# Key/value projection in quarters between the modulation blocks of a two-layer diffusion backbone, with weights stored as tiles

## The reference

```python
sh1, sc1, g1, sh2, sc2, g2 = adaln(c[:, None, :], mod_w[l], mod_b[l])        # silu(c) @ mod_w + mod_b
csh1, csc1, cg1, csh2, csc2, cg2 = adaln(c_ctx, mod_w[l], mod_b[l])
pl = modulate(x, norm_mix_g[l], sh1, sc1) @ w_in                              # latent: q, k, v, conv
hc = modulate(xc, norm_mix_g[l], csh1, csc1)
pc = hc @ (w_in if ctx_full else w_in[:, KV_LO:KV_HI])                        # context: k and v only
...
h = jnp.sin(f_freq * (h @ f_w2 + f_b2)); h = h @ f_w3                         # filters of layer 1
window = jnp.exp(-t_norm[:, None] * jnp.abs(f_decay)[None, :]) + FILTER_MOD_SHIFT
kf = jnp.fft.rfft(k2, n=2 * n, axis=0)                                        # their spectrum
```

## Time and profile before

| | us |
|---|---|
| median of 3 runs | 2467.48 (2467.28 to 2470.25) |
| the profiled execution: its own time | 2467.65 |
| its span, first to last instruction | 2465.9 |
| PE busy | 2372.1 (96% of the span) |
| DVE busy | 1823.9 (74%) |
| ACT busy | 1015.1 (41%) |
| start, up to the first product of `U_KV` | 151.24 |
| end of `U_KV` and first product of the next unit | 198.91 |

### The profile page before, as it was taken

One profiled execution on the slowest core, in us unless ns is written; L12 is line 12 of the kernel. 1 busy time (PEld: TensorE's weight loads), 2 busy tenths in 40 slices (PEclk: granted clock), 3 DMA queues, 4 the chain that ended last, 5 costly groups with the idle time before them and its releaser, 6 DMA issues.

```text
span 2465.9 us, 37957 instructions
## 1 busy us (share of the span) xinstructions
PE 2372.1 (96%) x14656; PEld 2073.9 (84%) x14656; DVE 1823.9 (74%) x2439; ACT 1015.1 (41%) x963; POOL 0.2 (0%) x4
## 2 busy tenths in 40 slices
PE   6899799998999999999989999999899999999997
PEld 2369478997888888888889989999788888888887
DVE  3557769988888888888888777875878655665565
ACT  4432334434444444444443223233444444444444
POOL 0000000000000000000000000000000000000000
PEclk7789899998999999999999999999999999999999
DMA  9897178996888888888875566556677555555552
GB/s 355 279 327 284 51 267 326 344 339 242 303 292 312 321 299 302 298 320 316 294 260 183 208 225 220 197 196 211 216 283 267 185 190 203 187 178 194 193 189 102
DMA packets 266042, 613.82 MB, mean 249 GB/s; under 512 B 12208, under 2 KB 12336, under 8 KB 265456
## 3 DMA queue, kind: packets, MB, share of 16 engines
q1 hardware_dynamic: 260992, 602.08, 68.6%
q10 hardware_dynamic: 4912, 9.77, 1.1%
HBM read 605.51 MB, written 6.29 MB: 248 GB/s over the span
## 4 chain that ended last, share of the span: by engine, by line
PE 86%; DVE 6%; DMA 3%; ACT 2%; issue 1%; SPq 0%; DVEq 0%; ACTq 0%
PE acc L578 20%; PE aux L578 20%; PE acc L521 17%; PE acc L604 11%; PE aux L604 10%; PE aux L521 2%; PE aux L656 1%; DMA w_raw<-mod_first 1%; ACT w_hi L1401 1%; PE aux L829 1%; PE aux L850 1%; DMA w_raw<-od_w_in 1%; DMA scr<-k_freq 1%; PE aux L518 1%; DVE w_lo L884 1%
## 5 line engine op out<-in xcount | busy, mean ns | idle before, releaser
L884 DVE TENSOR_TENSOR w_lo<-w_raw,w_hi 128x2048 fp32r<-128x2048 f32 x372 | 849.6, 2290 | 260.1 <-ACT w_hi L1401 244.8
L1401 ACT ACTIVATE w_hi<-w_raw 128x2048 fp32r<-128x2048 f32 x372 | 710.1, 1912 | 625.1 <-PE acc L521 278.1
L578 PE MATMUL acc<-act_a,w_hi 128*128 128x512 f32 x1216 | 295.4, 396 | 6.7 <-issue 4.5
L578 PE MATMUL aux<-act_a,w_hi 128*128 128x512 f32 x1216 | 290.1, 391 | 0.0
L578 PEld LDWEIGHTS acc<-act_a,w_hi 128*128 128x128 f32 x1216 | 226.9, 191 | 53.5 <-issue 5.8
L521 PE MATMUL acc<-act_a,w_hi 128*128 128x256 f32 x1920 | 261.7, 287 | 6.1 <-DVE summed L924 3.6
L578 PEld LDWEIGHTS aux<-act_a,w_hi 128*128 128x128 f32 x1216 | 223.4, 188 | 43.3
L521 PEld LDWEIGHTS acc<-act_a,w_hi 128*128 128x128 f32 x1920 | 247.6, 194 | 9.4 <-issue 4.5
L578 PE MATMUL acc<-act_b,w_hi 128*128 128x512 f32 x1024 | 244.3, 391 | 0.0
L892 DVE SCALAR_TENSOR_TENSOR m_raw<-m_raw,wide 128x1024 f32<-128x1024 f32 x180 | 217.7, 1218 | 5.0 <-DMA m_raw<-mod_rest 4.7
L578 PEld LDWEIGHTS acc<-act_b,w_hi 128*128 128x128 f32 x1024 | 188.2, 188 | 36.4
(11 more groups left out here) (169 smaller groups left out, 2189.2 us busy)
## 6 DMA issues: line engine op xcount, KB each, us to landing
w_raw<-ffn_w SPq DMA_DIRECT2D x256, 1024.0 KB, 7.0
m_raw<-mod_rest SPq DMA_DIRECT2D x180, 512.0 KB, 6.4
scr<-mod_rest SPq DMA_DIRECT2D x140, 512.0 KB, 6.7
w_raw<-od_w_in SPq DMA_DIRECT2D x48, 1024.0 KB, 8.1
w_raw<-ev_w_in SPq DMA_DIRECT2D x36, 1024.0 KB, 9.2
w_raw<-mod_first SPq DMA_DIRECT2D x32, 1024.0 KB, 9.6
w_raw<-ev_w_out SPq DMA_DIRECT2D x16, 1024.0 KB, 10.0
w_raw<-od_w_out SPq DMA_DIRECT2D x16, 1024.0 KB, 5.1
```

The lines of the kernel that those rows point to most:

```text
L578: return pe.matmul(banks[:, ft, :], w_hi[:, kg % 2, kc * 512 + ft * P:kc * 512 + ft * P + P], rhs[:, k, :], start=(k == 0), stop=False)
L884: TT(w_lo[:, kg % 2, :], w_raw[:, kg, :], w_hi[:, kg % 2, :].bitcast(F32), ALU.subtract)\
L1401: return act.activation(out_, in_, func, **kw)
```

## The change

1. The order of loads becomes a list `PIECES`: the 32 quarters of `mod_first`, and among them the 4 quarters of `U_KV`, one behind each of the blocks 3, 5, 6 and 7. Piece `i` goes into slot `i % 4` once piece `i - 4` is used up; for a quarter of `U_KV` that is when DVE has made its `w_lo`.
2. The filters are made one part `j` per block, in blocks 0 to 3 (spectrum up to block 4); `U_KV` (`keys_values(kg, steps)`) follows in quarters, with the quarters of blocks 5 to 7 and their turns put between its matmuls.
3. The decay comes as one row of 16 KB; PE spreads it over the partitions (`spread_decay`, 8 matmuls of 128x512) and ACT takes the absolute value while copying (`take_decay`). Its load, `fw3` and `fwd` are issued ahead of the first block.
4. The modulation units hosted by units move one on: before 0, 1, 2 beside `U_KV` and the two query units, 3 in the attention and 8 in the next ten units; now 0 and 1 beside the query units, 2 in the attention and 9 in the next ten.
5. All block weights except `mod_rest` are stored as tiles: each quarter is 128 rows of 8 KB in one piece, where it was 512 rows of 2 KB.

```diff
+PIECES = []
+for _u in range(START):
+    PIECES += [(_u, _kg) for _kg in range(4)]
+    if _u in (3, 5, 6, 7):
+        PIECES.append((None, {3: 0, 5: 1, 6: 2, 7: 3}[_u]))
+SEQ = {p: i for i, p in enumerate(PIECES)}
-MU_ATTN = 3
-MU_MIX = 4
+MU_ATTN = 2
+MU_MIX = 3
...
+            def used_up(i):
+                u, kg = PIECES[i]
+                if u is None:
+                    sp.wait_ge(lo_done, kg + 1)
+                elif kg == 3:
+                    sp.wait_ge(row_full, u + 1)
                 else:
-                    sp.wait_ge(raw_used, u * 3 + (kg - 2))
+                    sp.wait_ge(raw_used, u * 3 + (kg + 1))
...
-                    sp.dma_start(w_raw[:, kg, :].rearrange("p (c n) -> p c n", c=4),
-                                 w[ds(row + kg * 512, 512), ds(col, 512)].rearrange("(c p) n -> p c n", p=P))\
-                        .then_inc(landed[kg], 16)
+                    sp.dma_start(w_raw[:, kg, :], w[ds(row + kg * across * P, P), :]).then_inc(landed[kg], 16)
...
+            def spread_decay(i):
+                for j in range(4):
+                    if i:
+                        pe.wait_ge(decay_made, j + 1)
+                    pe.matmul(aux[j][:, :], ones[0:1, :], decay_row[:, 4 * i + j, :], start=True, stop=True)\
+                        .then_inc(decay_full, 1)
...
+            def keys_values(kg, between=()):
+                pe.wait_ge(hi_done, kg + 1)
+                steps = list(between)
+                if kg == 3:
+                    for kc in range(4):
+                        pe.wait_ge(normed, 2 * (4 * kg + kc + 1))
+                        for ft in range(4):
+                            for a in (0, T):
+                                mm = products(ft, kc, 0, a)
+                else:
+                    pe.wait_ge(normed, 8 * kg + 8)
+                    for ft in range(4):
+                        for kc in range(4):
+                            for a in (0, T):
+                                mm = products(ft, kc, 0, a)
+                        if ft < 3 and steps:
+                            steps.pop(0)()
+                mm.then_inc(hi_used, 1)
+                pe.wait_ge(lo_done, kg + 1)
...
+            pe.wait_ge(kout_ready, 16)
+            keys_values(0, [rows_of(5, 0), rows_of(5, 1), rows_of(5, 2), lambda: mod_turn(4), rows_of(5, 3)])
+            keys_values(1, [lambda: mod_turn(5), rows_of(6, 0), rows_of(6, 1), rows_of(6, 2), rows_of(6, 3)])
+            keys_values(2, [lambda: mod_turn(6), rows_of(7, 0), rows_of(7, 1), rows_of(7, 2), rows_of(7, 3),
+                            lambda: mod_turn(7)])
+            keys_values(3)
...
+            row_copy(5)
+            hi(0, 1, True)
+            modulate(16, ctx_items(2))
             row_copy(6)
-            modulate(16, ctx_items(2))
-            spectrum_out(3)
+            hi(0, 2)
             row_copy(7)
-            hi(0, 0, True)
-            hi(0, 1, True)
             modulate(24, ctx_items(3))
-            act.dma_start(rope[:, 0:2 * T + P], rope_in).then_inc(rope_landed, 16)
-
-            body(U_KV)
+            hi(0, 3)
+            hi(1, 0)
+            hi(1, 1)
```

More of the change, by code:

```diff
@@ L424, in mods @@
                 return [(mu + m, i) for m, i in tiles]
-            def mod_block(u, first=False):
-                for kg in range(4):
-                    if not first:
-                        raw_free(u, kg)
-                    sp.dma_start(w_raw[:, kg, :].rearrange("p (c n) -> p c n", c=4),
-                                 mod_first[kg * 512:kg * 512 + 512, START_COLS[u] * 512:START_COLS[u] * 512 + 512]
-                                 .rearrange("(c p) n -> p c n", p=P)).then_inc(landed[kg], 16)
@@ L435, in _ @@
-            mod_block(0, True)
-            sp.dma_start(fw3[0:FHID, :, :], fw3_in).then_inc(w3_landed, 16)
-            sp.dma_start(decay[:, :, :], decay_in).then_inc(decay_landed, 16)
-            sp.dma_start(fwd_first, fwd_in).then_inc(fwd_landed, 16)
-            sp.dma_start(x[:, :, :], x_in).then_inc(x_landed, 16)
-            mod_block(1)
-            sp.dma_start(ctx_raw, ctx_in).then_inc(ctx_landed, 16)
-            for i in range(2, START):
-                mod_block(i)
-            unit(U_KV, ev_w_in, 0, ATTN_W, mods(0), first=True, slots=EARLY)
@@ L680, in mod_turn, with products @@
                 mm.then_inc(row_turned, 1)
-            for kg in range(4):
-                mod_rows(0, kg)
+            def keys_values(kg, between=()):
+                def products(ft, kc, part, a):
+                    k = 4 * kg + kc
+                    w = (w_hi, w_lo)[part][:, kg % 2, kc * 512 + ft * P:kc * 512 + ft * P + P]
+                    for i, rhs in enumerate((act_a, act_b)):
+                        mm = pe.matmul(aux[ft][:, i * T:i * T + T], w, rhs[:, k, a:a + T],
+                                       start=(k == 0 and part == 0 and a == 0 and i == 0), stop=(k == 15 and part == 1 and i == 1))
+                    return mm
+                pe.wait_ge(hi_done, kg + 1)
[6 more added lines that the diff above has]
+                                mm = products(ft, kc, 0, a)
+                else:
+                    pe.wait_ge(normed, 8 * kg + 8)
[7 more added lines that the diff above has]
+                pe.wait_ge(lo_done, kg + 1)
+                for ft in range(4):
+                    for kc in range(4):
+                        mm = products(ft, kc, 1, 0)
+                    if kg == 3:
+                        mm.then_inc(psum_full, 1)
+                if kg < 3:
+                    mm.then_inc(ws_free, 1)
+                for step in steps:
+                    step()
@@ L716, in _ @@
-            mod_turn(START - 1)
+            mod_rows(1, 0)
+            spectrum(0, (0, 1))
+            spectrum(0, (2, 3))
+            mod_turn(0)
+            mod_rows(1, 1)
+            mod_rows(1, 2)
+            filters(1, 0)
+            filters(1, 1)
+            mod_rows(1, 3)
+            pe.wait_ge(mc_ready, 1)
+            norm_sums(0, acc[2], 16)
+            mod_rows(2, 0)
+            spectrum(1, (0, 1))
+            mod_rows(2, 1)
+            spectrum(1, (2, 3))
+            norm_spread(0, acc[2][:, T:2 * T])
@@ new lines, in _ @@
+            mod_turn(1)
+            mod_rows(2, 2)
+            filters(2, 0)
+            filters(2, 1)
+            mod_rows(2, 3)
+            pe.wait_ge(mc_ready, 2)
+            norm_sums(1, acc[3], 16)
+            mod_rows(3, 0)
+            mod_rows(3, 1)
+            spectrum(2, (0, 1))
+            mod_rows(3, 2)
+            spectrum(2, (2, 3))
+            norm_spread(1, acc[3][:, T:2 * T])
+            mod_turn(2)
+            mod_rows(3, 3)
+            filters(3, 0)
+            filters(3, 1)
@@ L1250, in _ @@
             for j in range(2):
-                u, t = j * 3 + U_CONV, [share(j * 3 + n, 10, 8) for n in range(3)]
+                u, t = j * 3 + U_CONV, [share(j * 3 + n, 10, 9) for n in range(3)]
                 body(u, lambda: gate_c(j), None, MU_MIX, t[0])
@@ L1480, in _, with take_decay @@
                 f(wide[:, i * 512:i * 512 + 512], aux[i][:, :], ACT.Copy).then_inc(silu_wide, 1)
+            def take_decay(i):
+                for j in range(4):
+                    act.wait_ge(decay_full, 4 * i + j + 1)
+                    f(decay[:, i, j * 512:j * 512 + 512], aux[j][:, :], ACT.Abs).then_inc(decay_made, 1)
+            take_decay(0)
             act.wait_ge(arg_ready, 2)
@@ L1492, in windows @@
             def windows(j):
-                own.wait(own.done(f(decay[:, :, j * 512:j * 512 + 512], decay[:, :, j * 512:j * 512 + 512], ACT.Abs)))
+                act.wait_ge(decay_made, 8)
                 for tt in range(2):
@@ L1501, in windows, with spectrum_out @@
                     ins.then_inc(win_ready, 1)
-            def spectrum_out(j):
-                for r in range(4):
+            def spectrum_out(j, parts=range(4)):
+                for r in parts:
                     act.wait_ge(kf_full, j * 4 + (r + 1))
```

239 lines of the change are left out of this document (128 added, 111 removed).

## The result

| | kernel before | changed kernel |
|---|---|---|
| median of the runs shown first | 2468.86 us (4 runs, 2467.28 to 2470.53) | 2483.98 us (4 runs, 2479.25 to 2489.36) |
| ratio, 95% interval | | 1.0063 [1.005, 1.0076] |
| a second set of runs | 2468.17 us (19 runs) | 2480.35 us (5 runs), 1.0056 [1.0043, 1.0069] |
| profiled execution: time, span | 2467.65, 2465.9 us | 2479.25, 2477.5 us |

The changed kernel is slower by 12 to 15 us, 0.6%. The forecast was 2470.7 us with 2453 to 2481 as its range; the first median lies 3 us above the range, and "slower" had a chance of 0.33.

What follows compares the result with a forecast made beforehand. It took PE's work, waits and clock to bound the start, not loads. Start +4.2, hosting 0 and tiled weights -1.0 gave +3.2 us on 2467.65, rounded with the median to 2470.7 us, range 2453 to 2481.

Steps and rivals of the forecast that it cites:

- slower: Outcome of the whole kernel more than 0.2% (4.9 us) slower than before; chance 0.33.
- Q: Start of the first query unit's first product, behind `U_KV`; 198.91 us before, forecast 203.1, range 197 to 208.
- spreading: In the start, `spread_decay`'s 8 new matmuls: 10.5 us, the first four at full clock, the others at half.
- The wait of `filters(2, 0)` for ACT's copies: In the start, a new PE wait of about 5 us, the two copies standing behind ten squares of ctx.
- the waits for `w_hi`: In `U_KV`, PE waits twice 2.7 us behind ACT's row copies, then a bare tail of 9.9 us.
- the start, +4.2: Everything up to Q: 4.2 us later than before, new waits being as long as those they replace.
- piece 20: Block 4's last quarter, waiting for the first `U_KV` quarter's `w_lo`: 5 us wait, first `U_KV` product at 123.3 us.
- Behind Q: After Q, nine hosted units instead of eight in the ten units behind the attention: 0 us, up to +2.
- the tiled weights, -1.0, at best -5: In the long convolution, earlier landings shorten chains PE waits on: 1.0 us off, between 0 and 5.
- Clock full all through: Rival: nearly gapless PE keeps full clock in the start, Q at 185, 2453 us (2453 to 2464); chance 0.27.
- Clock low between the products: Rival: half clock for rows and turns within `U_KV`, up to 12.6 us more, 2476 to 2484; chance 0.23.
- Loads bind the start: Rival: PE only follows the loads, Q near 155; chance 0.05, shared with something lighter unseen.

Runs made afterwards that it cites:

- e12: The changed kernel once more, unaltered, for a second profile and median: 2480.35 us, ratio 1.0056 to the kernel before.
- e4: The changed kernel with the weights row-major again, all else as changed: 2480.64 us, ratio 1.0048 to the kernel before.
- e6: The changed kernel with modulation unit 0 hosted inside the start, so that the ten units host eight again, tiled weights kept: 2481.83 us.
- e1: The kernel before with only the hosting shifted as in the change, nine modulation units in the ten units: 2472.18 us, ratio 1.0016.
- e9: The changed kernel with row-major weights and modulation unit 0 hosted inside the start, leaving the new start alone: 2476.84 us, ratio 1.0037.
- e13: The kernel before hosting nine units in the ten units, their 72 weight tiles dealt anew over the units: 2468.72 us, ratio 1.0001.
- e11: The kernel before with tiled weights for `od_w_in` and `od_w_out` alone, the long convolution's: 2473.44 us, ratio 1.0024.
- e15: The changed kernel, row-major, 72 hosted tiles dealt anew, first `U_KV` quarter behind block 4 instead of 3: 2467.85 us, ratio 1.0.
- e14: e15 plus ACT's roundings of the key/value quarters moved ahead of its row copies: 2457.39 us, ratio 0.996 to the kernel before.
- the dealing: The 72 hosted weight tiles dealt 8, 8, 7, 8, 7, 6, 6, 7, 7, 8 over the ten units: 2468.72 us in e13, 2472.18 in e1.
- e2: The kernel before with all the change's weights tiled and nothing else changed: 2473.81 us, ratio 1.0022.
- both mends: First `U_KV` quarter behind block 4 instead of 3, and ACT's roundings ahead of its row copies, in the changed kernel; e14 with both: 2457.39 us.
- e16: e14 with tiled weights except row-major `od_w_in` and `od_w_out`: 2454.24 us, ratio 0.995 to the kernel before.

## Why the prediction was wrong

**Right: the order of events in the start.** The first product of `U_KV` 1.4 us from its forecast, Q 0.6 us. By steps: spreading took 12.6 us where I had 10.5: the first four matmuls, which I had put at full clock (3.7), took 5.43, the other four 7.19, the half clock that I had given them. In e12 the same matmuls took 3.67 and 7.14, as forecast. PE's timeline of the first profile:

```profile
14.62 5.43 PE L647 MATMUL aux<-early_a,tab 1*128 1x512 f32 x8 [0.21 <-ACT wide L1477]
...
21.80 7.19 PE L647 MATMUL aux<-early_a,tab 1*128 1x512 f32 x8
```

The wait of `filters(2, 0)` for ACT's copies was 4.1 us (5 forecast), that of block 4's last quarter 6.4 (5), and the waits for `w_hi` 13.2 in three, the longest 8.1 (2.7 twice and a tail of 9.9 in which it stands).

**Wrong by size: the start, +4.2.** In the profile it is +4.7 at Q, but the profiled executions of the changed kernel, e12, e4 and e6 were 4.3 to 4.8 us faster than their own medians. By medians, e4 less e1 gives 2480.64 - 2472.18 = 8.5 us for the start, and e9 8.7. The sum was made on one execution of the kernel before, whose start spreads too (-0.5 to +1.7 us in e13, e11 and e1, which have it unchanged but for hosting). That I kept the range wide, to Q 208, was right; that 203.1 was its middle was luck of the one profile. Where the slower executions lose their microseconds was not seen, since none was profiled; between the profiled ones it is the first 40 us, by when the clock falls and rises (e12, above). The forecast had priced one such course.

What makes the start slow is shown in part. The waits for `w_hi`: their place on ACT was worth 10.5 us by medians (e15 against e14). The wait for piece 20: of the 12.8 us between e4 and e15 the dealing explains 3.5 (e1 against e13), which leaves some 9 by medians, from sets of runs on two chips. The two profiles say less. e15 gains 7.2 us on e4 at 120 us, where e4 waits 7.1 us for piece 20, and has given back 5.2 by 160. Behind the same wait of 2.5 us for `w_hi`, the next 16 matmuls took 3.79 us in e15 and 2.16 in e4. The chains of e15 and of e4:

```profile
136.07 3.79 PE aux L710 x16
```

```profile
141.78 2.16 PE aux L707 x16
```

So what the displaced quarter alone costs stays open, between the 1.6 us at Q of the two profiles and the 9 of the medians.

**Wrong: "Behind Q", 0 and up to +2 for nine hosted units.** This is the step that failed. It is +4.2 alone and up to +5.8 in the changed kernel. I looked for the place by DVE's share in the windows and found a convolution unit in which DVE has no idle time and 1.7 us of slack. That unit did hold: PE loses nothing there. But the slack of one `w_lo` was the wrong measure. The place was the first output-projection unit, where an addition on DVE empties `acc` and PE waits for it. It had some 0.2 us of slack, and two tiles more stand ahead of it (e1). In the changed kernel DVE also waited 1.2 us for a tile held up in SP's queue. I had priced neither the work ahead of this addition nor the clock that PE loses behind a wait.

**Wrong in sign: the tiled weights, -1.0, at best -5.** They cost 5.8 us everywhere together (e2) and 5.3 in the long convolution alone (e11). I had seen the chain that costs PE its waits in the long convolution and assumed that all landings on it would come earlier. Only the weights' do. The other load on that chain, `k_freq` in ACT's queue, stays at 2 KB rows and lands later beside long ones (at most 10.5 us instead of 8.2). I had bounded this term with no end below nothing.

**The sum.** By medians, +8.5 for the start, +4.2 for hosting, +5.8 for the tiled weights: 18.5, where 12.2 to 15.1 were measured. They don't add up fully, and the changed kernel's own two medians differ by 3.6. In its profiles it is the long convolution that holds less with all parts together (+1.5 and +4.0, e2 +5.6). In the first of them PE's wait behind `k_freq` is 5.0 us where it was 1.4, but its wait for `summed` is 1.3 where it was 3.6; why was not settled. In pairs the parts do add up by medians: with e9's 8.7 for the start, start and hosting give 12.9 (e4 measured 12.6), start and tiled weights 14.5 (e6 13.8).

**The rivals.** Clock full all through: no, it was 0.84 up to 123 us. Clock low between the products (2477 to 2483) comes nearest by its number, but not by its reason: the stretch from 123 to 203 us had 0.90, and PE idled 13.9 of its 80 us. Loads bind the start: no, DMA 0.77. None of the rivals named a cost behind Q; the slower side of the forecast had only a clock in it. As for the first rival, that a PE without gaps keeps the full clock: e14, with few gaps from 118 us to Q, had 0.95 there, and e15, with its waits for `w_hi`, 0.86; but e12, e4 and the changed kernel all fell to 0.50 between 20 and 25 us with PE busy all the time.

## What to carry to other kernels

When work is shifted to an engine that hosts it "for free", don't ask whether the engine has time on average, nor in the unit with the least idle time: go to each place where another engine waits for it at a unit's end, and add up what it has to do ahead of that. Then read the issue queue whose loads wait for the slots that it frees. Three tiles in the wrong units cost 3.5 us, and dealt otherwise nothing.

Longer rows make a load faster and can make its neighbours in other queues slower. Before tiling a transfer, list the small loads that run beside it and look whether one of them is waited for; here the change lost 5 us where one is, and a gain of 3 us where none is could not be told from the spread.

A piece that is put ahead of others in an in-order queue is paid for by the one that needs its slot: the order that makes the next release early, both mends together, was worth 20 us by medians (e4 to e14, less 3.5 for the dealing).

## What the runs showed of the hardware

A load of 512 KB in rows of 2 KB, in ACT's queue, took at most 8.2 us beside weights in rows of 2 KB (the kernel before), and up to 10.5 us beside weights in rows of 8 KB (e2), at the same 210 GB/s in all. The longest landing was 7.6 to 8.2 us in the nine profiles with row-major `od_w_in`, and 9.7 to 10.5 us in the five with a tiled one. I had expected nothing of it. Quarters of the first modulation landed in 6.8 us where they were tiled (changed kernel) and in 8.1 where they were row-major (e4); in 6.9 (e16) and 7.7 (e14) behind both mends.

Matmuls that spread one row over 128 partitions, 512 wide, took 0.92 us each (3.67 for four, e12) and 1.8 at half clock (7.14 for four), and so no less than those of the spectrum, which sum over 128 rows (3.68 for four at full clock).

The start of one and the same kernel differs by 5 us between two executions (Q at 203.7 and 198.5), and some 3 us of this lie between 15 and 30 us, where the clock was 0.64 in the one and 0.80 in the other at first. From 1700 us on, the distance of any profile here to that of the kernel before changes by 1.2 us at most.
